# A two-layer decoder trunk in one launch: x and memory also loaded feature-major, and the first projection run chunk by chunk

## What is computed

```python
for l in range(DEPTH):                       # DEPTH = 2
    h = rms_norm(x, norm_mix[l])
    qkv = (h @ w_in[l]).reshape(B, S, 3, N_HEADS_MIX, HEAD_DIM)
    ...                                      # per-head norms, rotary, 16 heads of attention -> mix
    x = x + mix.reshape(B, S, MIX_WIDTH) @ w_out[l]
    x = x + memory_cross_attention(rms_norm(x, norm_cross[l]), rms_norm(mem, norm_mem[l]),
                                   w_mq[l], w_mkv[l], w_mo[l], qn_mem[l], kn_mem[l])
    x = x + swiglu(rms_norm(x, norm_ffn[l]), w_gate_up[l], w_down[l])
```

## Time and profile before

| | us |
|---|---|
| median of 3 runs | 686.25 (686.1 to 686.6) |
| span of the profiled execution | 684.7 |
| median less span (what lies around the span, and the spread of runs) | 1.55 |
| PE busy in the span | 676.3 |
| first filler matmul starts | 6.71 |
| transposes of keys for the memory attention in layer 0 (L1825) start | 129.79 |

### The profile page before, as it was taken

How to read it: one execution, slowest core, us unless ns; L and a number is a source line. 1 busy time by engine, 2 the same in 40 slices (tenths; PEclk the granted TensorE clock), 3 DMA queues, 4 the chain that set the end, 5 groups by cost and what they waited for, 6 DMA issues and landing times.

```text
span 684.7 us, 10697 instructions
## 1 busy us (share of the span) xinstructions
PE 676.3 (99%) x3746; PEld 563.6 (82%) x3746; DVE 499.6 (73%) x960; ACT 394.1 (58%) x647; POOL 105.8 (15%) x127
## 2 busy tenths in 40 slices
PE   8999999999999999999999999999999999999997
PEld 7787777878888888888888878778788888888886
DVE  5799977587766666666678798875877666666665
ACT  6977776477544444444566669664865444444442
POOL 5254020236000000000034230202620000000000
PEclk9999999999999999999999999999999999999999
DMA  9945542146666666666547535214366666666631
GB/s 322 324 147 185 166 143 62 62 124 184 185 184 184 184 184 188 186 196 196 193 146 247 192 115 185 93 58 119 101 186 207 194 190 195 193 186 184 184 122 62
DMA packets 121392, 115.65 MB, mean 169 GB/s; under 512 B 2704, under 2 KB 95376, under 8 KB 121360
## 3 DMA queue, kind: packets, MB, share of 16 engines
q1 hardware_dynamic: 120784, 114.31, 53.8%
q10 hardware_dynamic: 576, 0.93, 0.4%
HBM read 114.17 MB, written 1.05 MB: 168 GB/s over the span
## 4 chain that ended last, share of the span: by engine, by line
PE 88%; DVE 5%; ACT 4%; DMA 1%; issue 1%; SPq 0%; POOL 0%; DVEq 0%; POOLq 0%; ACTq 0%
PE ps L1975 22%; PE ps L1582 19%; PE ps L1982 12%; PE ps L2023 6%; PE ps L2024 6%; PE ps L2025 6%; PE ps L1653 3%; DVE wlo L952 2%; PE ps L2004 2%; PE ps L1735 2%; PE ps L1908 2%; PE ps L1714 2%; PE ps L1771 1%; PE ps L1502 1%; DMA raw<-in_w_in 1%
## 5 line engine op out<-in xcount | busy, mean ns | idle before, releaser
L952 DVE TENSOR_TENSOR wlo<-raw,whi 128x2048 fp32r<-128x2048 f32 (+1 forms) x95 | 212.0, 2249 | 45.5 <-ACT whi L637 43.2
L637 ACT ACTIVATE whi<-raw 128x2048 fp32r<-128x2048 f32 (+1 forms) x102 | 188.5, 1875 | 11.7 <-PE ps L2025 6.5
L1975 PE MATMUL ps<-both,whi 128*128 128x512 f32 x672 | 167.2, 391 | 0.0
L1975 PEld LDWEIGHTS ps<-both,whi 128*128 128x128 f32 x672 | 123.4, 188 | 23.8
L1582 PE MATMUL ps<-whi,both 128*128 128x512 f32 x384 | 99.6, 395 | 1.8 <-ACT qkv L697 0.9
L1982 PEld LDWEIGHTS ps<-both,wlo 128*128 128x128 f32 x672 | 91.7, 190 | 6.5
L1982 PE MATMUL ps<-both,wlo 128*128 128x256 f32 x672 | 94.1, 283 | 0.0
L890 ACT ACTIVATE qkv<-ps 128x512 f32<-128x512 f32 x42 | 25.1, 598 | 112.7 <-PE ps L1982 112.7
L1582 PEld LDWEIGHTS ps<-whi,both 128*128 128x128 f32 x384 | 70.5, 188 | 17.7 <-ACT qkv L697 1.5
L2023 PE MATMUL ps<-whi,ahi 128*128 128x512 f32 x176 | 69.3, 394 | 0.0
L2024 PE MATMUL ps<-wlo,ahi 128*128 128x512 f32 x176 | 69.0, 392 | 0.0
(11 more groups left out here) (213 smaller groups left out, 873.9 us busy)
## 6 DMA issues: line engine op xcount, KB each, us to landing
raw<-in_w_gate_up SPq DMA_DIRECT2D x88, 512.0 KB, 5.0
raw<-in_w_in SPq DMA_DIRECT2D x23, 1024.0 KB, 5.5
raw<-in_w_down SPq DMA_DIRECT2D x22, 1024.0 KB, 5.0
raw<-in_w_out SPq DMA_DIRECT2D x8, 1024.0 KB, 5.0
raw<-in_w_mkv SPq DMA_DIRECT2D x4, 1024.0 KB, 5.2
raw<-in_w_mq SPq DMA_DIRECT2D x4, 512.0 KB, 3.5
raw<-in_w_mo SPq DMA_DIRECT2D x2, 1024.0 KB, 4.8
xs<-in_x SPq DMA_DIRECT2D x4, 256.0 KB, 5.5
```

What stands on the lines that cost most here:

```text
L637: ins = act.activation(whi[s][:, cols], raw[s][:, cols], ACT.Copy)
L952: ins = dve.tensor_tensor(wlo[s][:, cols], raw[s][:, cols], hi, ALU.subtract)
L1975: pe.matmul(ps[:, bank, :], whi[s][:, a:a + P], both[:, :, k, :], start=(k == 0), stop=False)
```

## The change

x is also laid out feature-major in memory by the host (`x_columns`, one 128x256 block for each of eight row blocks; the first is part of `starter`), and so is memory (`mem_columns`). Neither is transposed on chip in layer 0 any more: ACT and DVE split them straight from the loaded tiles. The identity moves from `starter` into the later load `ident_turn`.

The first column block is no longer made in filler pieces: `first_products` takes row block k of x and weights as they land, with the three passes of block k-1 and k woven together, for both token tiles. All eight first weight pieces (256 KB each) are loaded one by one between the four loads of x columns, unit 2 in two halves. Token-major x (two loads of 512 KB) stands behind unit 3 in SP's queue, feature-major memory behind unit 5, and token-major memory, which overwrites it, behind unit 10 and a wait for the last memory split.

With token-major x later, ACT does for layer 0: split of unit 3 (g = 6), sine (g = 7), squares of x (g = 8), `chunk_out(0,0)` (g = 9), split of unit 4 (g = 11, was 12), `chunk_out(0,1)` (g = 12). DVE asks for the root and takes it at g = 8; POOL makes that root behind the products with the sine and the lambda products. The splits of memory move from g = 19..22 to 28..31, its squares from 40 to 50, its root from 52 to 62.

```diff
-                        if layer == u == 0:
-                            for k in range(4):
-                                sp.dma_start(view(0, 4)[:, k, :], w_in[:, k, 512 * c:512 * c + 512]).then_inc(s_first[k].sem, 16)
-                            for q in FIRST_ORDER[1:]:
-                                x_quarter(q)
+                        cols = slice(512 * c, 512 * c + 512)
+                        if layer == 0 and u < 2:
+                            for k in range(4 * u, 4 * u + 4):
+                                sp.dma_start(view(u, 4)[:, k % 4, :], w_in[:, k, cols]).then_inc(s_first[k].sem, 16)
+                                for n, (at, chunks) in enumerate(X_COLUMN_LOADS):
+                                    if k == at:
+                                        x_columns(n, chunks)
                             continue
-                        load(layer, u, [(view(u, 4), w_in[:, 4 * h:4 * h + 4, 512 * c:512 * c + 512])])
-                        if layer == 0 and u == RING:
+                        if layer == 0 and u == 2:
+                            for half in range(2):
+                                sp.dma_start(view(u, 4)[:, 2 * half:2 * half + 2, :], w_in[:, 2 * half:2 * half + 2, cols])\
+                                  .then_inc(s_third[half].sem, 16)
+                            continue
+                        load(layer, u, [(view(u, 4), w_in[:, 4 * h:4 * h + 4, cols])])
+                        if layer == 0 and u == X_AFTER:
+                            for t in range(T):
+                                sp.dma_start(xs[:, t, :], x_in[:, t, :]).then_inc(s_x[t].sem, 16)
+                        if layer == 0 and u == MEM_COLUMNS_AFTER:
+                            sp.dma_start(mem_sb[:].rearrange("p t d -> p (t d)"), consts["mem_columns"]).then_inc(s_memT.sem, 16)
+                        if layer == 0 and u == MEM_AFTER:
+                            sp.wait_ge(m_lo.sem, 4)
                             sp.dma_start(mem_sb[:], mem.rearrange("b (t p) d -> p (b t) d", p=P)).then_inc(s_mem.sem, 16)
                 for h in range(2):
                     load(layer, U_MKV + h, [(view(U_MKV + h, 4), w_mkv[:, 4 * h:4 * h + 4, :])])
...
             pool.wait_ge(s_ones.sem, 1)
             for layer in range(DEPTH):
-                root(0, T)
-                if layer == 0:
+                if layer:
+                    root(0, T)
+                else:
                     pool.wait_ge(s_sin.sem, 1)
                     pool.wait_ge(s_rot.sem, 16)
                     pool.tensor_tensor(k_col[:], g_col[:, :, 0, :], g_col[:, :, 1, :], ALU.mult)
@@ -578,9 +598,9 @@
                 rope_q_scaled(0)
                 rope_k(1)
                 rope_q_raw(1)
+                rope_q_scaled(1)
                 if layer == 0:
                     root(0, T)
-                rope_q_scaled(1)
                 pool.wait_ge(sub_var.sem, sub_var.at(layer, 1))
...
+                if k == 0:
+                    act.wait_ge(s_starter.sem, 16)
+                for n, (_, chunks) in enumerate(X_COLUMN_LOADS):
+                    if k == chunks[0]:
+                        act.wait_ge(s_xcols[n].sem, 16)
+                act.activation(thi[:, k, :], x_cols[k], ACT.Copy, scale=g_rows[:, 0, G_MIX, k:k + 1]).then_inc(first_x_hi.sem, 1)
+            def first_weights(k):
+                s, cols = k // 4, slice(512 * (k % 4), 512 * (k % 4) + 512)
+                act.wait_ge(s_first[k].sem, 16)
+                ins = act.activation(whi[s][:, cols], raw[s][:, cols], ACT.Copy)
+                if k % 4 == 3:
+                    ins.then_inc(hi_done[s].sem, 1)
+                else:
+                    ins.then_inc((first_hi, second_hi)[s].sem, 1)
             def mem_hi(q):
-                act.wait_ge(m_ps.sem, q + 1)
-                act.activation(quarter(mhi, q), bank_as_chunks(MEM_BANKS[q]), ACT.Copy).then_inc(m_hi.sem, 1)
+                if q == 0:
+                    act.wait_ge(s_memT.sem, 16)
+                act.activation(two_chunks(mhi, q), two_chunks(mem_cols, q), ACT.Copy).then_inc(m_hi.sem, 1)
             def squares_of_x(layer, n, t):
                 if layer == 0 and n == 0:
-                    for q in (2 * t, 2 * t + 1):
-                        act.wait_ge(s_x[q].sem, 16)
+                    act.wait_ge(s_x[t].sem, 16)
                 else:
...
                     act.dma_start(small[:].rearrange("p l n -> p (l n)"),
                                   gains["small"].to_broadcast((P, DEPTH * N_SMALL))).then_inc(s_small.sem, 16)
                 else:
                     for q in range(2 * T):
                         x_hi(layer, X_MIX, q)
-                for t in range(T):
-                    squares_of_x(layer, 0, t)
+                    for t in range(T):
+                        squares_of_x(layer, 0, t)
...
                        .then_inc(mkv_out.sem, 1)
                 for g in range(6, LAST + 1):
+                    if layer == 0 and g == SIN_AT:
+                        act.wait_ge(s_cs.sem, 1)
+                        act.activation(cs[:], ang, ACT.Sin).then_inc(s_sin.sem, 1)
+                    if layer == 0 and g == ROOTS_AT:
+                        for t in range(T):
+                            squares_of_x(layer, 0, t)
                     for i in range(NCHUNK):
                         for t in range(T):
...
                 link(ins)
+            def first_x(k):
...
             dve.wait_ge(s_starter.sem, 16)
             for layer in range(DEPTH):
                 if layer == 0:
-                    for k in range(2):
-                        cols = slice(512 * k, 512 * k + 512)
-                        dve.wait_ge(s_first[k].sem, 16)
-                        dve.tensor_copy(whi[0][:, cols], raw[0][:, cols]).then_inc(first_hi_dve.sem, 1)
-                    x_lo(layer, X_MIX, 0)
-                    for k in range(4):
-                        cols = slice(512 * k, 512 * k + 512)
-                        if k < 2:
-                            dve.wait_ge(first_hi_dve.sem, k + 1)
-                        elif k == 2:
-                            dve.wait_ge(first_hi.sem, 1)
-                        else:
-                            dve.wait_ge(hi_done[0].sem, 1)
-                        ins = dve.tensor_tensor(wlo[0][:, cols], raw[0][:, cols], whi[0][:, cols].bitcast(F32), ALU.subtract)
-                    ins.then_inc(lo_done[0].sem, 1)
-                if layer == 0:
-                    x_lo(0, X_MIX, FIRST_ORDER[1])
-                    x_lo(0, X_MIX, FIRST_ORDER[2])
-                    split_lo(0, 1)
-                    x_lo(0, X_MIX, FIRST_ORDER[3])
+                    dve.wait_ge(s_first[0].sem, 16)
+                    dve.tensor_copy(whi[0][:, 0:512], raw[0][:, 0:512]).then_inc(first_hi_dve.sem, 1)
+                    for k in range(KC):
+                        first_x(k)
+                        first_weights(k)
                 else:
                     for q in range(2, 4):
                         x_lo(layer, X_MIX, q)
-                ask_roots_of_x(layer, 0)
+                    ask_roots_of_x(layer, 0)
                 split_lo(layer, 2)
-                take_roots_of_x(layer, 0)
+                if layer:
...
                     variance((km_sq, by_head(sqc[:, :, 0:MEM_W], MEM_HEADS)), km_var)
                 for g in range(6, LAST + 1):
+                    if layer == 0 and g == ROOTS_AT:
+                        ask_roots_of_x(layer, 0)
+                        take_roots_of_x(layer, 0)
                     for q in range(4):
                         if layer == 0 and g == MEM_AT[q]:
                             mem_lo_part(q)
...
+            def first_products():
+                def step(k, part):
+                    s, cols = k // 4, slice(512 * (k % 4), 512 * (k % 4) + 512)
+                    if part == 0:
...
+                    for t in range(T):
+                        done.append(pe.matmul(ps[:, proj_bank(0, 0, t), :], x_part[:, k, t * P:(t + 1) * P], w_part[s][:, cols],
+                                              start=k == part == 0, stop=k == KC - 1 and part == 2))
+                    if part == 2 and k == KC - 1:
+                        done[0].then_inc(tile_done.sem, 1)
+                    if part == 2 and k % 4 == 3:
+                        done[1].then_inc(used[s].sem, 1)
+                step(0, 0)
+                step(0, 1)
+                for k in range(1, KC):
+                    step(k, 0)
+                    step(k - 1, 2)
+                    step(k, 1)
+                step(KC - 1, 2)
             for layer in range(DEPTH):
-                build_x(layer, X_MIX, 0 if layer == 0 else 1)
                 if layer == 0:
-                    warm_up(WARM[1])
...
@@ -2048,10 +2100,11 @@
 FILLERS = 12 * (NCHUNK + 1) + 9
 OUT1_EARLY = ((0, 0), (1, 0), (0, 1))
-WARM = (8, 3)
-FIRST_ORDER = (0, 2, 1, 3)
-FIRST_AT = (2, 4)
```

(9 more changed lines are left out.)

## The result

The changed kernel takes 690.18 us (median of four runs, 689.48 to 692.7) against 686.24 before: 1.0063 times as long, 95% interval 1.0049 to 1.0076. It is slower by 3.9 us where +1.85 was forecast. The profiled execution took 689.53 us, with a span of 687.7 against 684.7: +3.0 by these two spans. So there are two things to explain: why the spans differ by 3.0 and not by 1.9, and why the median lies 2.48 us above the span of the profiled execution, where the forecast took 1.55.

A forecast was written before the change was run, and what follows sets the result against it. PE, busy 676.3 of 684.7 us, was taken as the bound, with DVE and ACT setting the first softmaxes. +2.8 less 0.87 gave +1.9: span 686.6, plus 1.55, about 688.1 us; range for 8 in 10, 685.2 to 690.3.

The forecast's parts named there:

- so at 37.5 us DVE is where it was: DVE at `lam_dot`: 37.3 against 37.56 before, PE's 5.6 us of gain being gone by then in waits.
- First filler 5.3, first block 16.8: PE at the start: first filler at 5.3 us, 1.4 earlier, and first block done at 16.8, bounds 16.3 to 18.3.
- Unit 3 lands at 18.0: Load queue: unit 3's weights land at 18.0 us, 1.5 behind the 16.5 at which 5.3 MB are moved.
- Root and read-out at 25.4 and 25.5: POOL makes the root behind 3.1 us of products, at 25.4 (19.4 before); `chunk_out(0,0)` starts at 25.5 against 22.46.
- `lam_dot` at 37.3: DVE behind unit 5's split: `lam_dot` at 37.3 us against 37.56 before.
- Splits of memory 4 x 0.60 = 2.4: DVE, between query norm and head sums of g = 37: four splits take 2.4 us, making masks 2.2 late.
- The second transpose at 68.65: PE behind memory's squares and the first `probT_out`: second transpose at 68.6 to 68.7, 2.8 later than 65.80.
- Given back 0.87: PE's wait of 0.87 us at 74.45 for a late ACT copy goes away.
- Sum +1.9: Whole kernel: +2.8 less 0.87 gives +1.9 us, span 684.7 to 686.6; +2.5 if DVE's two-SBUF splits delay POOL's root.
- rival D: Late root at `chunk_out(0,0)`: each us of later landing or POOL work comes through whole; 689.7 and more, chance 0.10.
- the median stands 1.55 above the span: Whole kernel: 1.55 us added to the forecast span of 686.6, giving a median of 688.15.
- Rival E: First products bound by landings: first block ends at 18.3, not 16.8, with no effect at the end; within the other cases.

The follow-up runs named there:

- b3_sqlate: The kernel before with only memory's squares late (40 to 50, root 52 to 62), written over memory: 686.32 us, ratio 0.9997.
- x5_order: The changed kernel reordered: x before unit 3, its squares before unit 3's split, root before products, read-out before sine, splits 22, 23, 28, 29, squares 54: 686.94 us.
- x2_root: The changed kernel with POOL's root of x put back ahead of the sine and lambda products: 689.55 us, ratio 1.0053.
- x4_all: The changed kernel with root ahead of the products, memory's splits at 21, 22, 22, 23 and its squares at 54: 689.32 us, ratio 1.0041.
- x8_clock_sq: The changed kernel with idle products in four TensorE gaps and memory's squares at 54 instead of 50: 689.49 us, ratio 1.0044.
- x7_clock: The changed kernel with idle products in four TensorE gaps of the first layer, each filling shorter than its gap: 691.37 us, ratio 1.0069.
- x3_splits: The changed kernel with memory's splits moved from 28 to 31 to 21, 22, 22, 23: 690.94 us, ratio 1.0064.
- b2_rootlate: The kernel before with only the root's order changed, behind the sine and lambda products: 692.92 us, ratio 1.0099.
- x6_warm: The changed kernel with early root, early memory splits, squares at 54, and idle TensorE products ahead of steps 31 and 32: 688.47 us, ratio 1.0028.
- x1_squares: The changed kernel with memory's squares on ACT moved from 50 to 54: 690.09 us, ratio 1.0057.
- y1_again: The changed kernel measured once more, unchanged: 689.89 us, ratio 1.0051 to the kernel before.
- y3_order3: The changed kernel with x, its squares, root and first read-out moved ahead, splits at 22, 23, 28, 29, squares at 60, their root at 67: 688.16 us.
- x9_order2: The changed kernel with x, its squares, root and read-out moved ahead, two memory splits at 38 and 39, squares at 60, their root at 67: 689.47 us.
- y2_clock_again: The changed kernel with idle products in four TensorE gaps, measured once more, unchanged: 690.64 us, ratio 1.0061.
- y4_columns_late: The changed kernel with x's columns of chunks 2 and 3 loaded behind the third weight chunk instead of the second: 689.48 us, ratio 1.0042.

## Where the prediction held, and which step failed

The direction held, and so did the path: a late first read-out, which no gap behind it takes up. The sizes on that path failed, and so did what the forecast charged to memory's splits and squares. Each line of the table is one profiled execution: the start of the first read-out, of the first mask, of the key transposes, and the two differences.

| kernel | read-out | mask | keys | mask - read-out | keys - mask |
|---|---|---|---|---|---|
| before | 22.46 | 56.12 | 129.79 | 33.66 | 73.67 |
| b3_sqlate | 22.08 | 55.74 | 129.15 | 33.66 | 73.41 |
| x5_order | 23.16 | 57.26 | 130.43 | 34.10 | 73.17 |
| x2_root | 25.40 | 58.80 | 132.07 | 33.40 | 73.27 |
| x4_all | 25.38 | 59.37 | 132.54 | 33.99 | 73.17 |
| after | 26.33 | 59.66 | 132.93 | 33.33 | 73.27 |
| x8_clock_sq | 26.41 | 59.73 | 132.89 | 33.32 | 73.16 |
| x7_clock | 27.68 | 61.00 | 134.28 | 33.32 | 73.28 |
| x3_splits | 27.83 | 61.22 | 134.49 | 33.39 | 73.27 |
| b2_rootlate | 27.24 | 62.07 | 135.74 | 34.83 | 73.67 |
| x6_warm | 24.97 | 58.45 | 131.65 | 33.48 | 73.20 |
| x1_squares | 27.02 | 60.31 | 133.46 | 33.29 | 73.15 |
| y1_again | 26.74 | 60.03 | 133.35 | 33.29 | 73.32 |
| y3_order3 | 22.89 | 56.98 | 131.45 | 34.09 | 74.47 |
| x9_order2 | 24.47 | 60.59 | 135.11 | 36.12 | 74.52 |

From the first mask to the keys it is 73.2 to 73.7 us, and 73.2 or 73.3 in the changed kernel, squares at 50 or at 54, clock down or not. Only the two kernels with the squares at 60, x9_order2 and y3_order3, lie 1.2 above. From read-out to mask it is 33.3 to 34.1 in the table but for two, b2_rootlate and x9_order2, whose long waits are told above. So within these kernels the loss follows the first read-out. It came 3.87 us late, the masks 3.54, the keys 3.14. x2_root (0.93 earlier, 0.86 less at the keys) and x7_clock (1.35 later, 1.35 more) move it in both directions.

The step that failed is the one that ends in "so at 37.5 us DVE is where it was", with the price of the splits behind it. Step by step. *First filler 5.3, first block 16.8*: 5.19 and 16.57. *Unit 3 lands at 18.0*: its split began at 18.07. *Sine to 21.5, squares to 23.6*: 21.64 and 23.72. *Root and read-out at 25.4 and 25.5*: 26.04 and 26.33, the first term that was too small. POOL's products began 0.3 late and took 3.45 us instead of 3.1, and the copy and its hand-over took 0.3 instead of 0.1. *`lam_dot` at 37.3*: 38.16, the same 0.86; DVE was not where it was (37.56) but 0.6 later. *Splits of memory 4 x 0.60 = 2.4*: 3.16, 0.79 each, the second term that was too small. They stand beside POOL's query rotations and read two SBUF tiles; in x9_order2, with POOL idle, two took 1.40, 0.70 each. *Masks at 58.3*: 59.66. *The second transpose at 68.65*: 70.14. *Given back 0.87*: from the second transpose to the keys 1.20 was given back (63.99 us before, 62.79 after), the wait of 0.87 and 0.33 more. *Sum +1.9*: +3.0 by the spans. The masks were 1.36 and the second transpose 1.49 later than forecast, which the two terms, 0.86 and 0.76, account for within 0.3; less the 0.33 this is the missing 1.1.

Two steps had about the right outcome for a wrong reason. The forecast charged the splits with the 2.2 us by which the masks were late, and the squares with the 0.6 on top. But x3_splits and x6_warm show that the splits moved ahead give nothing back. From read-out to keys it is 106.60 us in after, and with the squares later 106.48 in x8_clock_sq and 106.44 in x1_squares: they cost 0.1 to 0.2. DVE's share in it is in the windows view, DVE alone (stretch, length, busy us and count, granted clock, DMA share, GB/s): from the read-out to `lam_dot` and from there to the masks, of before, then of after.

```profile
22.46:37.56 15.10, 12.19 (x21) 1.00 0.74 251
37.56:56.12 18.56, 16.61 (x38) 1.00 0.58 194
```

```profile
26.33:38.16 11.83, 8.89 (x18) 1.00 0.73 267
38.16:59.66 21.50, 18.50 (x40) 1.00 0.50 164
```

In the first stretch DVE is idle for 2.9 us in both, but has 3.3 less to do: unit 3's low part is done ahead of the late read-out, and two memory splits are gone. In the second it has 1.9 more to do, all four of the splits, and 1.05 more to wait. The sum of both is -0.3; the late root is what is left. What the splits cost, against a kernel that had them for nothing, no run shows, since at either place something waits for them.

The median, 690.18, is near the upper end of the stated 685.2 to 690.3 and lies in the range of rival D (689.7 and more, chance 0.10), whose mechanism is the late root, coming through whole for each us that a load lands later or POOL takes more. That it comes through whole was right. In the profiled execution unit 3 came as forecast, so its share was POOL and the hand-overs, 0.8; late landings add to it in other executions.

The median was missed by 2.1, of which this is 1.1. The other 0.9 is the term "the median stands 1.55 above the span", which measured 2.48. It mixed two things. The later runs of the kernel before list time and span side by side: the time is 2.2 above the span (1.8 in after and in all that were made from it; why is open), and the spans are 683.9 to 684.8, mostly 684.3 or 684.4. So 684.7 came from one of its longer executions, and 687.7 from a shorter one of after, whose nine runs have a median span of 688.1. The spans of typical executions differ by some 3.7.

The spread has grown too. Before, 15 runs of one session lie within 0.7 us, but the nine runs of after in two sessions go from 689.3 to 692.7. Its first products and everything up to the root start at landings, and these differ between executions. Unit 3's split at 18.07, 18.25, 18.30, 18.48 and 19.43 (after, y2_clock_again, y4_columns_late, y1_again, x7_clock) goes with keys at 132.93, 133.08, 133.13, 133.35 and 134.28. Rival E, landings that bind the first products, was put aside as without effect on the end, since PE waits near 28 us anyway. It has one, because unit 3's load waits for unit 0's splits, and so the root does. That the longer runs of after are executions with late landings was argued from this, not seen: only one execution of a kernel has a trace. 692.7 lies beyond the one late landing that was traced, and stays open.

The Trainium skill (GPSIMD Engine Reference, Specifications) says that POOL shares its SBUF interfaces with DVE and contends with DVE instructions that have two SBUF inputs. By that rule the forecast gave +2.5 instead of +1.9, for a root 0.6 later. The trace agrees on the contention: the first product behind the sine took 0.59 us (0.21 in the earlier trace rows) and ended at 22.37, when unit 3's low part ended at 22.31. That is 0.38 of the 0.64 by which the root was late against 25.4; the rest is hand-overs and the sine, so the size of 0.6 came out right in part by luck. The rows of before, with one operand in PSUM, were too low a price for the splits as well.

## What to carry to other kernels

When work is taken from the engine that is full, look first for the earliest hand-over that the other engines need, here the root behind the sine, and price the change by how far it moves that instruction; work moved about within the queues behind it gained nothing here, and in two orders it cost 1.2 and 2.5 us against x5_order. Where a changed operation is priced by rows of another operand kind (PSUM before, SBUF after) and a neighbour is shown to be held up by that kind, take the upper bound. A start that is made to hang on landings also makes the time wider, so the median is not the profiled execution plus a constant; compare medians of spans with medians of spans.

## What the runs showed of the hardware

A DVE weight split of two SBUF operands (128x2048, 2.28 us) all but stopped POOL for its whole length: operations of 0.32 and 0.46 us took 2.36 to 2.51 in x4_all, x5_order and x9_order2, twice in a row where two splits followed one another. Four of POOL's operations for the angles, beside unit 2's split (15.58 to 18.24), took 4.28 us instead of 2.35; that was hidden behind ACT. DVE lost too: that split took 2.66 us, unit 3's 2.29.

```profile
14.96 4.28 POOL L513 TENSOR_TENSOR probT<-probT 128x160 f32<-128x160 f32 x4
```

TensorE's granted clock went down to half, from 2.4 to 1.2 GHz, behind gaps, for 2 to 7 us: in x1_squares behind gaps of 1.34 and 1.82 us with 1.2 us of work between them, in y1_again behind 1.77 and 0.55, in b2_rootlate in a single one of 4.88. It happened in some executions of a kernel and not in others: y1_again is the kernel after, whose first profile has gaps of 1.84 and 0.55 at the same place and the clock at 1.0. Stretches 41 to 43, 43 to 45 and 45 to 47 us of x1_squares (length, busy us and count, granted clock, DMA share, GB/s):

```profile
41.00:43.00 2.00, 1.00 (x5) 0.51 1.00 386
43.00:45.00 2.00, 2.00 (x8) 0.50 0.25 94
45.00:47.00 2.00, 2.00 (x6) 0.50 0.28 22
```

It cost next to nothing where a wait for ACT or DVE came behind it, since TensorE used that wait up (y1_again waits 1.80 before its second transpose, after 2.10), and some 0.5 us in x4_all, by the comparison with x6_warm.

The first loads of one and the same kernel completed 1.2 us apart (x7_clock and y2_clock_again: ACT takes up the second load of x's columns at 7.72 and 6.51), and 1.35 apart in x7_clock and after, which don't differ up to there. The rates are nearly equal: 368 GB/s in after and 363 in x7_clock between 6 and 8 us, 387 and 396 between 12 and 14. Which of the 16 engines was behind isn't shown.
